# Two-block model on one core: memory keys and values of both layers made beside the RWKV prepare stage, and the layer's row norm, turn and split taken into its wide projection

## The reference, cut to what matters

```python
for l in range(2):                               # second block, x: 512 x 1024, mem: 256 x 1024
    h = _rmsnorm(x, norm_g[l])
    z = h @ w_in[l]                              # split into q, k, v, gates of three branches
    ...
    mem_kv = _rmsnorm(mem, mem_norm_g[l]) @ w_mem_kv[l]        # 256 x 1024
    # in _memory_xattn: k, v = halves of mem_kv as 4 heads of 128; k = _rmsnorm(k, mem_k_norm[l])
    o_m = _memory_xattn(mem_q, mem_kv, mem_q_norm[l], mem_k_norm[l]) * silu(mem_silu)
    g = sigmoid(merge_g)
    u = g[:, :, 0] * (o_a @ w_branch_a[l]) + g[:, :, 1] * (o_b @ w_branch_b[l]) + g[:, :, 2] * (o_m @ w_branch_m[l])
    x = x + u @ w_out[l]
```

## Time and profile before

| what | value |
|---|---|
| runs | 3: 4143.44, 4141.07, 4134.83 us |
| median | 4141.07 us |
| profiled execution, its own time | 4140.19 us |
| its span in the trace | 4138.4 us |
| mean granted TensorE clock | 0.887 |
| PE busy | 3342.1 us (81%) |
| DVE busy | 1549.7 us (37%) |
| ACT busy | 1009.2 us (24%) |
| DMA, mean over the span | 153 GB/s, 634.91 MB |
| first instruction of the first layer | 2353.50 us into the span |

### The profile page before, as it was taken

How to read it: one execution, slowest core, us unless ns; L and a number is a source line. 1 busy time by engine, 2 the same in 40 slices (tenths; PEclk the granted TensorE clock), 3 DMA queues, 4 the chain that set the end, 5 groups by cost and what they waited for, 6 DMA issues and landing times. The chain is left out here.

```text
span 4138.4 us, 63900 instructions
## 1 busy us (share of the span) xinstructions
PE 3342.1 (81%) x25339; PEld 2140.0 (52%) x25340; DVE 1549.7 (37%) x2533; ACT 1009.2 (24%) x1762; POOL 146.8 (4%) x222
## 2 busy tenths in 40 slices
PE   4897585576799988999999459977698479878797
PEld 1775474475332322333333148764587368655685
DVE  5536656656211101111111337335533245436332
ACT  1332212212111111111111123334422223425322
POOL 0000000002100000000000100000000000000000
PEclk8998687787799999999999679977899789969898
DMA  9530000004779999979879423120131133200321
GB/s 347 191 112 2 2 3 2 2 3 160 275 273 376 345 403 399 390 287 398 312 264 382 153 92 93 51 43 1 61 102 61 65 92 99 48 1 1 102 82 61
DMA packets 248601, 634.91 MB, mean 153 GB/s; under 512 B 30036, under 2 KB 69716, under 8 KB 247732
## 3 DMA queue, kind: packets, MB, share of 16 engines
q1 hardware_dynamic: 231058, 584.73, 39.3%
q10 hardware_dynamic: 11092, 25.68, 1.7%
q0 software_dynamic: 6224, 21.24, 1.6%
HBM read 591.48 MB, written 40.11 MB: 153 GB/s over the span
## 5 line engine op out<-in xcount | busy, mean ns | idle before, releaser
L1485 PE MATMUL ps<-raw,ex_xT 128*64 128x512 f32 x3072 | 702.3, 601 | 34.3 <-DMA raw<-in_w_dram 34.2
L1485 PEld LDWEIGHTS ps<-raw,ex_xT 128*64 128x64 f32 x3072 | 205.6, 137 | 437.3 <-issue 364.9
L1576 DVE TENSOR_SCALAR ex_gl<-ps 128x256 f32<-128x256 f32 x96 | 40.7, 424 | 1043.5 <-PE ps L1485 1043.5
L1485 PE MATMUL ps<-raw,ex_aT 128*64 128x512 f32 x1536 | 353.2, 597 | 13.7 <-DMA raw<-in_w_dram 12.7
L1485 PEld LDWEIGHTS ps<-raw,ex_aT 128*64 128x64 f32 x1536 | 104.0, 136 | 217.5 <-issue 185.0
L1807 PE MATMUL ps<-zhi,hh_z 128*128 128x512 f32 (+1 forms) x448 | 170.3, 380 | 29.7 <-DVE zlo L1915 29.7
L2368 PE MATMUL ps<-uhi,u_hh 128*128 128x512 f32 x384 | 151.1, 394 | 49.8 <-DVE ulo L2414 49.8
L2414 DVE TENSOR_TENSOR ulo<-oT,uhi 128x2048 fp32r<-128x2048 f32 x36 | 82.5, 2293 | 255.9 <-ACT uhi L2391 255.9
L1808 PE MATMUL ps<-zlo,hh_z 128*128 128x512 f32 (+1 forms) x448 | 169.8, 379 | 0.0
L1809 PE MATMUL ps<-zhi,hl_z 128*128 128x512 f32 (+1 forms) x448 | 169.6, 379 | 0.0
L2369 PE MATMUL ps<-ulo,u_hh 128*128 128x512 f32 x384 | 150.7, 392 | 0.0
(11 more groups left out here) (565 smaller groups left out, 6403.5 us busy)
## 6 DMA issues: line engine op xcount, KB each, us to landing
raw<-in_w_dram SPq DMA_DIRECT2D x384, 1024.0 KB, 18.4
oT<-in_w_in_dram SPq DMA_DIRECT2D x64, 512.0 KB, 3.7
mT<-in_w_ada_dram SPq DMA_DIRECT2D x12, 2048.0 KB, 16.4
oT<-in_w_in_dram SPq DMA_DIRECT2D x24, 1024.0 KB, 5.2
expert_out<-xn SPq DMA_DIRECT2D x4, 4096.0 KB, 16.5
expert_out<-ex_yrow ACTq DMA_DIRECT2D x98, 128.0 KB, 6.3
modb<-in_w_in_dram SPq DMA_DIRECT2D x10, 1024.0 KB, 6.6
oT<-in_w_mem_kv_dram SPq DMA_DIRECT2D x8, 1024.0 KB, 6.2
```

Source lines behind the costliest of these rows:

```text
L1485: mm = pe.matmul(o, x, M["raw"][:, slot, k, h * 512:(h + 1) * 512], start=(s >= 8 and kk == 0), stop=(kk == 7))
```

## The change

Keys and values of the memory, for both layers, are made in the first block and kept in DRAM; a layer loads them when it needs them. The row norm, turn and split of `x` no longer have stages of their own but run inside `project_z`, and their result stays in SBUF until `merge`.

- `fourier` loads `mem` and the two memory gains, PE turns it (16 transposes, four at a time: groups 0 and 1 ahead of the position matmuls, 2 and 3 between them), DVE multiplies each turned block with the gain of each layer (16 products), and SP stores the turned rows of both layers (2 MB) and waits for it. The row factors `memrs` are made on DVE and ACT.
- `rwkv_prepare`, in each of its four rounds, loads the turned rows of both layers (2 MB) and one head's columns of `w_mem_kv` (4 x 512 KB), does 32 matmuls of 256 columns in plain float32 ahead of the `rk` sums, ACT takes them out with the row factor, and SP stores four slices of 128 KB and waits for them.
- `mix_out` loads the keys of both layers and norms them on DVE (with a root on ACT) ahead of its gating. `settle` turns them (16 transposes at the head of PE's list, four copies on ACT between the root and the rows' normalisation) and stores them on ACT's queue. `EARLY` goes from 10 to 9.
- The ten stages of a layer's head go. `project_z` begins with the squares, root, scaling, 32 transposes and the split of `x`'s rows, and the six small gains are loaded behind its sixth piece. `compressed_attention` loads keys and values (1 MB). The split ahead of `merge` has `oT` alone.

The instructions of an engine at the places that matter, in the order of its list (line, operation, output and inputs, size, and how often it repeats), before and after:

The diff, cut to what the prediction speaks of:

```diff
-EARLY = 10
+EARLY = 9
...
+        @block.sync
+        def _(sp):
+            for l in range(LAYERS):
+                sp.dma_start(W["memT"][:, l, :, :], memt[l]).then_inc(kv_in[l], 16)
+                w = A["w_mem_kv_2"][l].rearrange("(k p) (s h d) -> p k s h d", p=P, s=2, h=4)
+                for part in range(2):
+                    sp.dma_start(W["wkv"][:, l, :, part, :], w[:, :, part, c, :]).then_inc(kv_in[l], 16)
+            sp.wait_ge(kv_out, 2 * LAYERS)
+            for l in range(LAYERS):
+                for part in range(2):
+                    sp.dma_start(kvrows[l, part].rearrange("(m p) (h d) -> p m h d", p=P, h=4)[:, :, c, :],
+                                 W["kvout"][:, l, :, part * P:(part + 1) * P]).then_inc(kv_kept, 16)
+            sp.wait_ge(kv_kept, 32 * LAYERS)
...
+            pe.wait_ge(sig, 3)
+            for l in range(LAYERS):
+                pe.wait_ge(kv_in[l], 48)
+                for m in range(2):
+                    for k in range(KD):
+                        last = pe.matmul(ps[:, 4 + l, m * 256:(m + 1) * 256], W["memT"][:, l, k, m * P:(m + 1) * P],
+                                         W["wkv"][:, l, k, :, :].rearrange("p s d -> p (s d)"), start=(k == 0), stop=(k == KD - 1))
+                last.then_inc(kv_prod, 1)
...
+            for l in range(LAYERS):
+                act.wait_ge(kv_prod, l + 1)
+                for m in range(2):
+                    act.activation(W["kvout"][:, l, m, :], ps[:, 4 + l, m * 256:(m + 1) * 256], ACT.Copy,
+                                   scale=T["memrs"][:, m:m + 1]).then_inc(kv_out, 1)
...
+        @block.sync
+        def _(sp):
+            sp.dma_start(Y["mem"][:, :, :], A["mem_2"][0].rearrange("(m p) d -> p m d", p=P)).then_inc(mem_in, 16)
+            for l in range(LAYERS):
+                sp.dma_start(Y["mg"][:, l, :], A["mem_norm_g_2"][l].rearrange("(k p) -> p k", p=P)).then_inc(mg_in, 16)
+            sp.wait_ge(mt_out, 16)
+            for l in range(LAYERS):
+                sp.dma_start(memt[l], Y["memT"][:, l, :, :]).then_inc(memt_kept, 16)
+            sp.wait_ge(memt_kept, 16 * LAYERS)
...
+            done(dve.tensor_tensor(Y["sq"][:, :, :], Y["mem"][:, :, :], Y["mem"][:, :, :], ALU.mult))
+            done(dve.tensor_reduce(T["memrs"][:, :], Y["sq"][:, :, :], AX_X, ALU.add))
+            dve.tensor_scalar(T["memrs"][:, :], T["memrs"][:, :], 1.0 / D, RMS_EPS, ALU.mult, ALU.add).then_inc(mean_in, 1)
+            dve.wait_ge(mg_in, 16 * LAYERS)
+            turned_rows(0)
+            turned_rows(1)
+            dve.wait_ge(root, 1)
+            done(dve.reciprocal(T["memrs"][:, :], T["memrs"][:, :]))
+            turned_rows(2)
+            turned_rows(3)
...
+            def turn_rows(g):
+                for k in range(2):
+                    for m in range(2):
+                        at = (2 * g + k) * P
+                        last = pe.transpose(ps[:, 2 + g % 2, (2 * k + m) * P:(2 * k + m + 1) * P], Y["mem"][:, m, at:at + P], T["s"]("ident"))
+                last.then_inc(mt, 1)
+            pe.wait_ge(mem_in, 16)
+            turn_rows(0)
+            turn_rows(1)
...
+                if 1 <= j <= 2:
+                    pe.wait_ge(mt_out, 4 * j)
+                    turn_rows(j + 1)
...
+            dve.wait_ge(kv_in, 32 * LAYERS)
+            done(dve.tensor_tensor(sq, heads, heads, ALU.mult))
+            done(dve.tensor_reduce(N["kr"][:, :], sq, AX_X, ALU.add))
+            dve.tensor_scalar(N["kr"][:, :], N["kr"][:, :], 1.0 / P, RMS_EPS, ALU.mult, ALU.add).then_inc(kv_mean, 1)
+            dve.wait_ge(kv_root, 1)
+            done(dve.reciprocal(N["kr"][:, :], N["kr"][:, :]))
+            done(dve.tensor_tensor(heads, heads, bc(N["kr"][:, :], 2, P), ALU.mult))
+            for l in range(LAYERS):
+                done(dve.tensor_tensor(heads[:, 8 * l:8 * l + 8, :], heads[:, 8 * l:8 * l + 8, :], bc(N["mkg"][:, l, :], 1, 8), ALU.mult))
...
+            for i in range(2 * LAYERS):
+                for j in range(2):
+                    for m in range(2):
+                        at = (2 * (i % 2) + j) * P
+                        mm = pe.transpose(ps[:, 4 + i, (2 * j + m) * P:(2 * j + m + 1) * P], N["kvr"][:, 2 * (i // 2) + m, at:at + P], S("ident"))
+                mm.then_inc(kt, 1)
...
+            for i in range(2 * LAYERS):
+                act.wait_ge(kt, i + 1)
+                act.activation(N["kmT"][:, i * 512:(i + 1) * 512], ps[:, 4 + i, :], ACT.Copy).then_inc(kt_out, 1)
...
+            act.wait_ge(kt_out, 2 * LAYERS)
+            for l in range(LAYERS):
+                act.dma_start(kmt[l].rearrange("p h t -> p (h t)"), N["kmT"][:, l * 1024:(l + 1) * 1024]).then_inc(kt_saved, 16)
...
+            for t in range(TT):
+                pe.wait_ge(h_ready, t + 1)
+                for k in range(KD):
+                    last = pe.transpose(ps[:, 2 * t + k // 4, (k % 4) * P:(k % 4) * P + P], X["h"][:, t, k * P:(k + 1) * P], S("ident"))
+                last.then_inc(h_turned, 1)
             for q in range(count):
                 n, part = q // parts, q % parts
...
+            for t in range(TT):
+                if t:
+                    act.wait_ge(sums, t)
+                act.activation(X["tmp"][:, :], x[:, t, :], ACT.Square, accum_out=ss[:, t:t + 1]).then_inc(sums, 1)
+            act.wait_ge(row_mean, 1)
+            act.activation(ss[:, 0:TT], ss[:, 0:TT], ACT.Sqrt).then_inc(row_root, 1)
             for q in range(min(nh, count)):
                 high(q)
+            for t in range(TT):
+                act.wait_ge(h_turned, t + 1)
+                act.activation(hi_t[:, :, t * P:(t + 1) * P], turned_tile(t), ACT.Copy).then_inc(row_hi, 1)
...
+            def scaled_rows(t):
+                dve.scalar_tensor_tensor(out=X["h"][:, t, :], in0=x[:, t, :], scalar=ss[:, t:t + 1], in1=X["ng"][:, :],
+                                         op0=ALU.mult, op1=ALU.mult).then_inc(h_ready, 1)
+            def low_rows(t):
+                dve.wait_ge(row_hi, t + 1)
+                at = slice(t * P, (t + 1) * P)
+                dve.tensor_tensor(lo_t[:, :, at], turned_tile(t), hi_t[:, :, at].bitcast(F32), ALU.subtract).then_inc(row_lo, 1)
+            dve.wait_ge(sums, TT)
+            dve.tensor_scalar(ss[:, 0:TT], ss[:, 0:TT], 1.0 / D, RMS_EPS, ALU.mult, ALU.add).then_inc(row_mean, 1)
+            dve.wait_ge(row_root, 1)
+            done(dve.reciprocal(ss[:, 0:TT], ss[:, 0:TT]))
+            dve.wait_ge(gain_in, 16)
+            for t in range(TT):
+                scaled_rows(t)
+            low(0)
+            for t in range(TT):
+                low_rows(t)
+            for q in range(1, min(nh, count)):
                 low(q)
...
+        @block.sync
+        def _(sp):
+            for dst, src in loads:
+                sp.dma_start(dst, src).then_inc(loaded, 16)
+            sp.wait_ge(loaded, 16 * len(loads))
...
-            load_stage(nc, [(mem[:, :, :], A["mem_2"][0].rearrange("(t p) d -> p t d", p=P)),
-                            (ng[:, :], A["norm_g_2"][l].partition_broadcast(P)), (mg[:, :], A["mem_norm_g_2"][l].partition_broadcast(P)),
...
-            with stage(nc, "scaled") as (block, scaled):
...
-            rms_rows(nc, mem, mem, mg[:, :], tmp, ss, 2)
-            rms_rows(nc, h, x, ng[:, :], tmp, ss, TT)
-            turn(nc, bank, ident, tiles4(memT, lambda t, c: mem[:, t, c * P:(c + 1) * P], KD, 2)
-                 + tiles4(hT, lambda t, c: h[:, t, c * P:(c + 1) * P], KD, TT))
-            mh, ml = sb(s, "memh", [P, KD, 256], F32R), sb(s, "meml", [P, KD, 256], F32R)
-            split_stage(nc, split_jobs(memT, mh, ml, KD, 4))
-            w = A["w_mem_kv_2"][l].rearrange("(k p) n -> p k n", p=P)
-            split_gemm(nc, ps, lambda n: w[:, :, n * 512:(n + 1) * 512], lambda n: 512, 2, 2,
-                      lambda k, m: mh[:, k, m * P:(m + 1) * P], lambda k, m: ml[:, k, m * P:(m + 1) * P], *split_ring(s, sb, "m", oT, 4, 2),
...
-            head_norms(nc, [(km, [(km, km)], L["mkg"][:, :], P)], h[:, :, :].rearrange("p a b -> p (a b)"), r)
-            turn(nc, bank, ident, tiles4(kmT, lambda t, c: kv[:, t, c * P:(c + 1) * P], 4, 2))
...
-                hh, hl = sb(s, "hh_z", [P, KD, SEQ], F32R), sb(s, "hl_z", [P, KD, SEQ], F32R)
-                split_stage(nc, split_jobs(hT, hh, hl, KD))
+                X = {n: sb(s, "in_" + n, shape) for n, shape in {"h": [P, TT, D], "ng": [P, D], "tmp": [P, D]}.items()}
...
-                project_z(nc, ps, T, L, A["w_in_2"][l].rearrange("(k p) n -> p k n", p=P), Z, silu, oT[:, 10:12, :], sq, r,
-                          hh, hl, *zring)
+                project_z(nc, A, l, ps, T, L, x, X, ss, Z, silu, oT[:, 10:12, :], sq, r, hh, hl, *zring)
...
-                    compressed_attention(nc, ps, T, Z)
+                    compressed_attention(nc, ps, T, Z, [(kmT, kmt[l]), (vm, kvrows[l, 1].rearrange("(m p) n -> p m n", p=P))])
...
+            for n in ("oh", "ol"):
```

(6 more changed lines are left out.)

188 lines of the change are left out of this document (90 added, 98 removed).

## The result

| | runs | median us | lowest to highest |
|---|---|---|---|
| before | 4 | 4142.05 | 4134.83 to 4143.44 |
| changed | 4 | 3976.84 | 3974.79 to 3980.73 |

The ratio is 0.9607, with a 95% interval of 0.9595 to 0.9619. Forecast were 3957 (0.956) with 3945 to 3979 around it. The time lies inside that range, but outside the forecast's own (3947 to 3968): the change brought 165 us where 184 were expected. The profiled execution took 3977.78 us, its span is 3976.0, so 162.4 us less than the span before.

The account below looks back on a forecast made before the run. The layers' heads (107.9 and 105.2 us) were taken as bound only by their order, the experts as full on PE. Terms summed to -183.5 from 4140.2, giving 3957 us; own range 3947 to 3968, eight in ten 3945 to 3979.

Parts of the forecast that it names:

- The heads: Both layers' starts: all but 15.8 us before the first wide-projection matmul goes, 92.1 and 89.4 us, together -181.5.
- Rival (c): Layer heads: ACT's row copies wait behind its weight copies if first weights land late; +10 each layer, 3977; chance 0.07.
- The split ahead of `merge`: Ahead of merge in both layers: the first four pieces, 4.63 us on DVE, go; -9.2 for two layers.
- `fourier`: Fourier stage: 16 transposes lengthen PE's chain, the 2 MB store barely hides, eight semaphores come; +2.0, bounds 0.5 and 5.
- `settle`: In settle: four ACT copies at 0.60 between root and normalisation, less DVE's 0.4, give +2.2; with semaphores +2.4.
- `mix_out`, `EARLY`: Key norm hides in DVE's wait for PE: 0, at worst 3; EARLY at 9: 0, at worst 2.5.
- `rwkv_prepare`: Four prepare stages: new loads, 32 matmuls (13.7 us), copies and stores hide beside DVE's chain; 0 but for semaphores, 1.3.
- rival (a): In rwkv_prepare: loads at half the rate outlast DVE's chain, 4.2 us late times four, +17, 3974; chance 0.12.
- Rival (b): In rwkv_prepare: new float32 matmuls take four passes, 8 us for each round, +32, 3989; chance 0.03.
- Rival (d): Rest of the layers: PE's granted clock drops to half in full-clock matmul stretches; 4141 and more; chance 0.02.
- The rounds: Four RWKV rounds: only five new semaphores in each rwkv_prepare show, at 0.065 us each, +1.3.
- prepare rounds longer than before by more than 1 us: In rwkv_prepare: a sign named beforehand that would show the forecast wrong.

Follow-up runs that it names:

- e4: Changed kernel without the loads and 32 matmuls of the memory's keys and values in the four prepare stages; 3982.8 us, ratio 0.9623.
- e6: Changed kernel with 704 bytes left free ahead of the wide projection's weight parts and 1600 ahead of those of merge and w_out; 3968.2 us, ratio 0.9570.
- e7: Changed kernel with the edits of e5 and e6 together; 3961.6 us, ratio 0.9562.
- e9: Changed kernel with all rounded and rest parts of the layers at multiples of 256 bytes from each other, row factors in unused columns; 3963.0 us, ratio 0.9564.
- e5: Changed kernel with the row factors memrs in unused columns of an existing tensor; 3979.6 us, ratio 0.9603.
- e14: Kernel before with 32 bytes left free behind onerow, so that all placed later lies 32 bytes further on; 4141.6 us, ratio 1.0005.
- e8: Kernel before with 320 bytes left free ahead of the projection's weight parts and 448 ahead of those of merge and w_out; 4167.6 us, ratio 1.0058.

## Why the forecast was 20 us off

- **The heads** (-181.5): right, 15.1 and 15.7 us to the first product where 15.8 were summed, -182.5 in all. Rival (c) fell: ACT's weight copies ended at 2379.0, before the first tile was turned.
- **The split ahead of `merge`** (-9.2): -9.2. **`fourier`** (+2.0): +1.3. **`settle`** (+2.4): +2.5. **`mix_out`, `EARLY`** (0): 0.5, and no loss in `experts`.
- **`rwkv_prepare`** (0 but for semaphores): the stage is as long as before, so rival (a) fell. The loads were never waited for: in all four rounds the new matmuls start right behind L589, in the first at 339.63, which is 9.5 us after the stage's start (I had 14.7). In the kernel before, the `rk` sums begin at 350.32; the 353.53 that I had is the start of their second group. And the price of a matmul came from a misread row. In the earlier trace rows the row of L572 stands for x2 of 128x256 in 1.06, and I took it for two matmuls at 0.43. The program has one there, which the trace records twice: at half clock it took 0.85. The 32 new ones are x64 for the same reason. They took 13.98, or 0.437 each, because the granted clock was at its upper level and not at half. The windows over them, changed, and over the same place before:

```profile
340.00:354.00 14.00, 13.61 (x64) 11.63 (x62) 12.78 (x11) 4.67 (x7) 0.00 (x0) 1.00 0.31 78
```

```profile
336.00:350.00 14.00, 0.47 (x2) 0.00 (x0) 12.65 (x11) 5.45 (x8) 0.00 (x0) 0.62 0.00 0
```

  Two errors cancelled, so that the forecast of 13.7 us was luck. In the third round even this is just enough: the `rk` sums start at 675.66, as the matmuls end. The rule of the Trainium skill that I had weighed and put aside ("FP8 and Floating Point Precision", section "TensorE Precision Notes": true float32 takes four passes) was right: four times 256 columns at 2.4 GHz are an estimated 0.427 us, and 0.437 was measured. Rival (b) failed not by the passes but by the clock. It had risen to 1.00 at 337.5, before the matmuls, and stayed there to 358.0; before the change it rose at 336.6 as well and fell to 0.50 at 340.0, with PE idle, and in e4, without the matmuls, at 344.0. They kept the clock up.
- **Rival (d), the clock:** the granted clock did the opposite of what it feared. It is 0.907 over the span, where it was 0.887.
- **What failed** is a term that the sum doesn't have: the layers' matmuls were held at the pace that they had before. The 0.227 us a matmul "in the full-clock pace" was read from operands in step, and the change moved `hh` and `hl` out of it, to 0.2333 and 0.2289. In the table the layers outside heads and splits are 15.1 us longer where 1.4 were summed; the stages that e6, e7 and e9 bring back give some 15 us, the medians of e5 and e7 18.0. No row of before could show it, but the change's new order of buffers could have been laid beside the old one; the forecast went by the order of instructions and their waits alone.
- **The front** (0): +3.5, by the loads' targets 32 bytes further on (e14). The sum had no term for it either.
- **The rounds** (+1.3): +8.9, and the forecast's own sign of being wrong, "prepare rounds longer than before by more than 1 us", came true. Four to five of these come and go with the added instructions (1.0 of them is the semaphores at the stages' ends); the rest stays open, and so does the cause.
- **`experts`, `combine`** (0): -1.8; no run tells why.

The two best versions, e7 with 3961.6 and e9 with 3963.0 us, have ratios of 0.9562 and 0.9564 to the kernel before of the same hour, and the forecast was 0.956: by the whole time they can't be told from it, although their rounds are 635.5 and 640.2 us long. What makes up for the rounds in them was not followed.

## What to carry to other kernels

A change that moves buffers can change the pace of matmuls it never touches: after a change in allocation, compare the count of matmuls in a full window at full clock, and the duration of one by line, before looking for waits. Keep the two operands of long rows of float32r matmuls like these a multiple of 256 bytes apart, for instance by placing small tensors ahead of the large ones and not between them. And where a row joins records, hold its count against the program's, before a price is taken from it.

## What the hardware showed that wasn't expected

- A float32r matmul of 128x512 with a new 128x128 weight each time starts every 0.2267 us at full clock if moving and standing operand are a multiple of 256 bytes apart, and every 0.2289, 0.2325 and 0.2333 if the moving one lies 64, 128 and 192 bytes beyond such a multiple: up to 3%, and 24.6 us in this kernel (e8).
- Loads of 2 MB with the DMA engines full ran at 386 GB/s into targets 32 or 64 bytes further on than before (seven profiles), against 400 to 412 (nine).
- 32 plain float32 matmuls, put where PE had been idle and the granted clock had fallen from 1.00 to 0.50 (a mean of 0.62), kept it at 1.00 and took 13.98 us.
